# Even layer's normed heads: attention weights transposed by the DMA as halfword planes instead of by TensorE

## The reference

```python
proj = jnp.einsum('bsd,de->bse', u, w_in_even[i])
qa, ka, va, qb, kb, vb, gate = jnp.split(proj, even_splits, axis=-1)
qa = apply_axial_rope(rms_norm_2(qa.reshape(b, s, A_HEADS, HEAD_DIM), a_q_norm_g[i]), rope_tables)
ka = apply_axial_rope(rms_norm_2(ka.reshape(b, s, A_KV_HEADS, HEAD_DIM), a_k_norm_g[i]), rope_tables)
ya = gqa_attention(qa, ka, va)          # softmax(q k / sqrt(128)) v, 8 heads, 2 key/value heads
yb = diff_attention(...)                # 8 differential heads
y = jnp.concatenate([ya, yb], axis=-1) * jax.nn.silu(gate)
h = h + jnp.einsum('bse,ed->bsd', y, w_out_even[i])
```

## Time and profile before

| | us |
|---|---|
| median of 3 runs | 3058.57 (3057.92 to 3058.85) |
| the profiled execution | 3058.66 |
| its span, first to last instruction | 3056.9 |
| TensorE busy | 3043.0 |
| VectorE busy | 1869.1 |
| ScalarE busy | 1469.8 |
| POOL busy | 134.2 |

### The profile page before, as it was taken

One profiled execution on the slowest core, in us unless ns is written; L12 is line 12 of the kernel. 1 busy time (PEld: TensorE's weight loads), 2 busy tenths in 40 slices (PEclk: granted clock), 3 DMA queues, 4 the chain that ended last, 5 costly groups with the idle time before them and its releaser, 6 DMA issues.

```text
span 3056.9 us, 48305 instructions
## 1 busy us (share of the span) xinstructions
PE 3043.0 (100%) x20906; PEld 2827.8 (93%) x20906; DVE 1869.1 (61%) x2263; ACT 1469.8 (48%) x1699; POOL 134.2 (4%) x132
## 2 busy tenths in 40 slices
PE   9999999999999999999999999999999999999999
PEld 9989999999999999989888888889998889999987
DVE  7775555445445557776565565556787666767663
ACT  5544433333333357755443443345565654555553
POOL 0001000000000011110000000002000001101000
PEclk9999999999999999999999999999999999999999
DMA  6334555555554554455555555554444545555554
GB/s 236 108 111 166 174 173 178 179 177 171 176 179 168 182 195 176 159 193 179 194 191 188 185 179 198 187 192 179 179 140 153 178 175 184 179 193 186 174 191 152
DMA packets 94516, 539.57 MB, mean 177 GB/s; under 512 B 25568, under 2 KB 26080, under 8 KB 31584
## 3 DMA queue, kind: packets, MB, share of 16 engines
q1 hardware_dynamic: 77264, 532.14, 50.0%
q10 hardware_dynamic: 17040, 4.34, 0.8%
HBM read 530.15 MB, written 2.10 MB: 174 GB/s over the span
## 4 chain that ended last, share of the span: by engine, by line
PE 97%; DVE 1%; ACT 1%; DMA 1%; issue 0%; SPq 0%; ACTq 0%; DVEq 0%
PE PB L1158 28%; PE PB L1159 15%; PE PB L1183 14%; PE PB L1182 14%; PE PB L1184 13%; PE PB L1177 2%; PE PB L1178 2%; PE PB L1179 2%; PE PB L1169 1%; PE PB L1168 1%; PE PB L1167 1%; PE PB L1240 1%; DMA raw<-in_mla_in 1%; PE PB L1308 1%; DVE WLt L1796 0%; PE PB L1309 0%
## 5 line engine op out<-in xcount | busy, mean ns | idle before, releaser
L1796 DVE TENSOR_TENSOR WLt<-raw,WHt 128x2048 fp32r<-128x2048 f32 (+2 forms) x506 | 1139.3, 2259 | 760.7 <-ACT WHt L1415 760.2
L1415 ACT ACTIVATE WHt<-raw 128x2048 fp32r<-128x2048 f32 (+2 forms) x506 | 955.0, 1890 | 1117.3 <-PE PB L1159 582.0
L1158 PE MATMUL PB<-Xt,WHt 128*128 128x512 f32 x2880 | 1027.6, 395 | 0.0
L1159 PE MATMUL PB<-Xt,WLt 128*128 128x256 f32 x2880 | 808.5, 281 | 0.0
L1158 PEld LDWEIGHTS PB<-Xt,WHt 128*128 128x128 f32 x2880 | 540.8, 188 | 109.8
L1182 PE MATMUL PB<-Xt,WHt 128*128 128x272 f32 (+1 forms) x2192 | 635.0, 290 | 2.8 <-DVE WLt L1796 1.9
L1183 PE MATMUL PB<-Xt,WHt 128*128 128x272 f32 (+1 forms) x2192 | 630.2, 287 | 0.0
L1184 PE MATMUL PB<-Xt,WLt 128*128 128x272 f32 (+1 forms) x2192 | 626.9, 286 | 0.0
L1159 PEld LDWEIGHTS PB<-Xt,WLt 128*128 128x128 f32 x2880 | 543.5, 189 | 0.1
L1182 PEld LDWEIGHTS PB<-Xt,WHt 128*128 128x128 f32 x2192 | 412.8, 188 | 12.6 <-DVE WLt L1796 4.9
L1183 PEld LDWEIGHTS PB<-Xt,WHt 128*128 128x128 f32 x2192 | 413.5, 189 | 1.1 <-issue 0.2
(11 more groups left out here) (268 smaller groups left out, 2858.1 us busy)
## 6 DMA issues: line engine op xcount, KB each, us to landing
raw<-in_gu SPq DMA_DIRECT2D x176, 1024.0 KB, 4.8
raw<-in_dn SPq DMA_DIRECT2D x88, 1024.0 KB, 4.8
raw<-in_odd_in SPq DMA_DIRECT2D x64, 1024.0 KB, 4.8
raw<-in_even_in SPq DMA_DIRECT2D x52, 1024.0 KB, 4.9
raw<-in_lru_in SPq DMA_DIRECT2D x24, 1024.0 KB, 4.9
raw<-in_mla_o SPq DMA_DIRECT2D x16, 1024.0 KB, 4.8
raw<-in_lru_o SPq DMA_DIRECT2D x16, 1024.0 KB, 5.0
raw<-in_even_o SPq DMA_DIRECT2D x16, 1024.0 KB, 4.9
```

The costliest lines, as they stand in the source:

```text
L1158: t.matmul(o, wh, both, start=first, stop=False)
L1159: m = t.matmul(o[:, 0, :], wl, ah, start=False, stop=last)
L1415: a.activation(hi, r, ACT.Copy).then_inc(s_hi, 1)
L1796: v.tensor_tensor(lo, r, hi.bitcast(f32), sub).then_inc(s_lo, 1)
```

## The change

In the eight normed heads of the even layer the weights of a head are no longer transposed by TensorE. ScalarE copies them as two planes of halfwords into `EVEN_PLANES` (`even_planes`), a DMA on ScalarE's queue transposes them into `EVEN_CROSSED` (`even_cross`), two ScalarE copies put the halves together in `EVEN_WOVEN`, a third rounds them to `TTH`, and VectorE takes the rest to `TTL` (`even_weave`). Both planes are woven by ScalarE, where the odd layer has one on VectorE and the split into planes on POOL. `E1` is free once the planes are copied.

The steps of group q stand elsewhere. Head 2q: planes at the end of unit 2, crossing inside unit 3 before block 2, weave at the end of unit 4, values at the end of unit 5. Head 2q + 1: scores inside unit 3 before block 2, planes at the end of unit 4 (behind the next group's `q_step`; for q = 3 on their own), crossing at the end of unit 5, ahead of the values of head 2q, weave at the end of unit 6, values inside unit 7 before block 1. `weigh_split` now waits for `TTL`. The functions `halfwords`, `weigh_split` and `q_step` are otherwise as before.

```diff
@@ plan @@
+    def even_planes(hd):
+        p.mark("even planes", "even planes", hd)
+        p.step("even_planes", hd)
+        now["E1"] = ("even planes", hd)
+
+    def even_weave(hd):
+        p.mark("even woven", "even woven", hd)
+        p.mark("trh", "trh", hd)
+        p.mark("trl", "trl", hd)
+        p.step("even_weave", hd, now["TT2"])
...
-        p.step("weigh_split", hd, vj, ("out", "tr", hd) if stage_[0] == "e" else ("trl", hd), vready)
+        p.step("weigh_split", hd, vj, ("trl", hd), vready)
...
             rope2(("qA", q), "q", q_in)
+            if q:
+                even_planes(("e", 2 * q - 1))
...
         p.after(0, q_step)
+        a, b = ("e", 2 * q), ("e", 2 * q + 1)
         if q == 0:
             p.inside(2, 1, lambda s=s: s(0))
         else:
             p.after(1, lambda s=s: s(0))
-        p.inside(3, 1, lambda s=s, q=q: (t_step(("e", 2 * q)), s(1)))
-        p.after(4, lambda v=v, q=q: (v(0), t_step(("e", 2 * q + 1))))
-        p.after(5, lambda v=v: v(1))
+        p.after(2, lambda a=a: even_planes(a))
+        p.inside(3, 2, lambda s=s, a=a: (p.step("even_cross", a), s(1)))
+        p.after(4, lambda a=a: even_weave(a))
+        if q == 3:
+            p.after(4, lambda b=b: even_planes(b))
+        p.after(5, lambda v=v, b=b: (p.step("even_cross", b), v(0)))
+        p.after(6, lambda b=b: even_weave(b))
+        p.inside(7, 1, lambda v=v: v(1))
@@ buffers @@
+        EVEN_PLANES, EVEN_CROSSED, EVEN_WOVEN = sqt[:, 0:512], acct[:, 0:512], buf["vA"]
+        s_even_crossed = ctx.enter_context(nc.semaphore("s_even_crossed"))
@@ TensorE, steps inside a unit @@
-                elif what == "turn_split":
-                    turn(a[0])
+                elif what == "weigh_split":
+                    weigh_split(*a)
@@ ScalarE @@
+            def even_planes(hd):
+                a.wait_ge(*when("pp", hd))
+                if hd[1]:
+                    a.wait_ge(s_even_crossed, 16 * hd[1])
+                a.activation(EVEN_PLANES.bitcast(u16).rearrange("p (a n) -> p a n", a=2), halfwords(E1),
+                             ACT.Copy).then_inc(sems["even planes"], 1)
+
+            def even_cross(hd):
+                a.wait_ge(*when("even planes", hd))
+                if hd[1]:
+                    a.wait_ge(*when("even woven", ("e", hd[1] - 1)))
+                x = EVEN_CROSSED.bitcast(u16).rearrange("p (g n) -> p g n", n=128)
+                a.dma_start(x, EVEN_PLANES.bitcast(u16), transpose=True).then_inc(s_even_crossed, 16)
+
+            def even_weave(hd, free):
+                a.wait_ge(s_even_crossed, 16 * (hd[1] + 1))
+                if hd[1]:
+                    a.wait_ge(*when("trl", ("e", hd[1] - 1)))
+                for i in range(2):
+                    x = EVEN_CROSSED.bitcast(u16)[:, 512 * i:512 * i + 512].rearrange("p (q k n) -> p k q n", q=2, k=2)
+                    w = EVEN_WOVEN.bitcast(u16).rearrange("p (k q n a) -> p a k q n", k=2, q=2, a=2)[:, i]
+                    m = a.activation(w, x, ACT.Copy)
+                m.then_inc(sems["even woven"], 1)
+                a.wait_ge(*when(*free))
+                a.wait_ge(*when("even woven", hd))
+                a.activation(TTH, EVEN_WOVEN, ACT.Copy).then_inc(sems["trh"], 1)
@@ VectorE @@
+            def even_weave(hd, free):
+                v.wait_ge(*when("trh", hd))
+                v.tensor_tensor(TTL, EVEN_WOVEN, TTH.bitcast(f32), sub).then_inc(sems["trl"], 1)
```

More of the change, by code:

```diff
@@ L1733, in _ @@
                     crossed(*x)
+                elif what == "even_planes":
+                    even_planes(*x)
+                elif what == "even_cross":
+                    even_cross(*x)
+                elif what == "even_weave":
+                    even_weave(*x)
                 elif what == "uq_out":
```

## The result

The changed kernel takes 3087.53 us (median of 4 runs, 3085.28 to 3088.86), the kernel before beside it 3058.24 (3057.31 to 3058.85): 1.0095 times as long, 95% interval 1.0083 to 1.0107. The prediction said slower, 3076.4 us and at most 3085: the direction is right, the size is not.

A forecast was written before the change was run, and what follows sets the result against it. TensorE was taken as the bound, busy 3043.0 of 3056.9 us. Transposes -3.5, old waits -0.7 and -0.2, values' waits +14.9, scores' waits +7.2 gave +17.7 us: 3076.4, range 3067 to 3085 (own forecast 3071 to 3082).

The forecast's parts named there:

- Each forecast wait: TensorE waits 3.6 us three times and 4.1 once before second heads' values, and 2.4 three times before first heads' scores.
- Only the waits of v: Rival: VectorE finishes its low part before the roots come, so the scores' 7.2 us falls away: 3069.2 us; 10 in 100.
- the other sign: Rival: second head's values and the scores don't wait, so only the gain of 4.2 us is left: 3054.5; 4 in 100.
- worth of the transposes: 32 TensorE transposes removed from the eight normed heads, 0.44 us per four, win 3.5 us.
- The clock falls in the waits: Rival: each of four waits for values puts TensorE's next unit at 1.2 GHz: +22.6 us, to 3099; 6 in 100.
- Other moves: Later scores, the release of E1 and SP's loads shift no wait of TensorE; nothing added to the sum.
- With each period 5 us longer, ScalarE and VectorE gain time: In the periods between groups, these two engines gain time because each period grows by 5 us.
- ScalarE becomes the bound: Rival: ScalarE about 81% busy per period; if lateness grows between groups, some 5 us more: 3081; 8 in 100.

The follow-up runs named there:

- E1: Not a run: a buffer of the kernel, free once ScalarE has copied the planes; it has no measured time of its own.
- the kernel with the roots first: Changed kernel with the first head's weave moved behind the next pair's roots and rotation on all engines (q = 1, 2, 3): 3080.32 us, 1.0075 times before.
- The two kernels with later values: Changed kernel with the second head's values before the unit's last quarter, or after the whole unit, instead of before the second quarter: 3085.41 and 3084.69 us.
- the waits filled: Changed kernel with 26 unread matmuls put in front of each wait for the second head's values: 3085.96 us, 1.0093 times before.
- the values after the whole unit: Changed kernel with the second head's values at the end of unit 7 instead of inside it before block 1: 3084.69 us, 1.0089 times before.

## Why the prediction was right and wrong

**Direction, and the waits: right.** Each forecast wait was met within 0.5 us; the sums are 14.2 for 14.9 and 7.1 for 7.2 us. The chain that gave them (boundary, weight copy, two halfword copies, rounding, low part) stands in ScalarE's rows as it was laid out. That the scores wait because the roots stand behind the first head's weave was shown by the kernel with the roots first, with the lists of ScalarE and VectorE changed together. "Only the waits of v" is refuted, and so is the other sign. The row of before also gave the right worth of the transposes: 32 at 0.11 us fit the ledger within 1.2 us, while at 0.275 us each the ledger would come out at 22.5, 4.1 under what was measured.

**"The clock falls in the waits" was taken for a rival of 6 in 100, with the forecast expecting 1.00.** This step failed, with 8.5 us. It was argued against with "the waits are short and TensorE is full around them"; no row of before has a wait of more than 0.6 us between full stretches in these 140 us, so the rows could not say that. What they had was the fall at the end. The size was wrong on the other side: the rival let the clock be low for a whole unit, 5.64 us per wait, while here the clock was back before the unit ended and a fall cost 1.7. The Trainium skill, "TensorE: Matmul & The Clock Gate", HAM oscillation, which says that idle gaps between bursts bring the lower clock back, agrees with the trace at the four waits of the values and the bank wait, and not at the three waits of the scores.

**The bank of head 7 was not looked at.** The part "Other moves" went over the releases of E1, the scores and SP's loads, and not over the banks, though values that come later release their bank later: this step failed too, with 2.4 us that the sum put at nothing. For seven heads that costs nothing in the changed kernel, for the eighth 2.4 us, and its fall of the clock 1.7 more.

**"With each period 5 us longer, ScalarE and VectorE gain time" is wrong in kind.** It holds for busy time, but VectorE's idle time stands at fixed places of its list, in front of the weave's low part, and what is behind doesn't gain by it. The two kernels with later values showed the consequence: I expected that taking a wait away gives back its length, and it gave back nothing. The period of a pair, from scores to scores, is 34.2 us in the kernel after (2228.66 to 2262.88), where about 32 was written, and 33.4 (2228.83 to 2262.26) with the values' waits removed. The rival "ScalarE becomes the bound" was nearest to this, but it named busy time, and ScalarE is busy 105.7 of 170 us (2190 to 2360), so it isn't full. Its lateness doesn't grow from pair to pair either: 3.42, 3.70, 3.44.

**The sum.** One rounding is off: 5.09 less 1.42 is 3.67 and not 3.6, which would have made the waits for values 15.1 and the forecast 17.9. 17.7 forecast; less 0.8 for waits that were shorter, plus 8.5 of clock and 2.4 of bank makes 27.8; 26.6 was measured in the profiled execution and 29.3 between the medians.

**What stays open.** Why the sum of waits and lost clock stays at 30 to 32 us is argued from the timelines: between the boundary ahead of the second head's weave and the next pair's scores the work goes to and fro between ScalarE and VectorE with hardly a gap that TensorE could shorten. It would be tested by putting the weave's copies ahead of the weight copy on ScalarE, or the low part behind the scaling on VectorE. No run here measured either, nor a kernel in which both kinds of wait are filled. What decides whether the clock falls after a given wait is open too. No version here is faster than the kernel before.

## What to carry to other kernels

A wait put into a matrix engine that was full costs its length and can bring a slower clock behind it: here five of eight waits of 2.2 to 3.7 us brought 1.7 us each. Where an engine takes its list in order, look for the late event in every list, not only in that of the bound engine, and ask what stands behind it there; taking the wait away where it showed only moved it here, to other things that this engine releases, banks above all. When a consumer is put later, follow its bank to the next user, for each instance by itself, the last one above all.

## What the runs showed of the hardware

- The granted clock fell to 0.50 (1.2 GHz) after waits of 1.81 to 5.15 us in a TensorE that was otherwise full, and came back by itself. A lone fall costs 1.7 us; behind the longest waits the loss by the windows is two or three times that (3.4 us behind the bank wait of 3.98 with the waits filled). The length of the wait alone doesn't decide: 2.16 us before scores had no fall in the kernel after (2262.88), and the same 2.16 us before the same scores had one with the values after the whole unit (2262.01; 0.50 in the window from 2264 us); 3.42 us before the values had one in the kernel after and none with the roots first.
- The fall can come behind the restart, or in the wait itself. In the kernel after TensorE starts at 2240.23, the next matmuls are at full spacing, and the slow ones begin at 2241.05, 0.8 us behind. In the kernel with filled waits the scores at 2261.96 are slow at once (1.09 us for two against 0.67). With the values after the whole unit the clock is 0.50 in the window from 2346 us, in which TensorE runs nothing.
- A transposing DMA of 128x1024 halfwords from SBUF to SBUF landed in 3.1 us (median of eight, 3.0 to 6.5), against 2.7 for the odd layer's; the weave's first copies (L1659) never stood idle for one.
- ScalarE copies 1024 halfwords per partition in 1.04 us, but 512 with strides in 0.76, so the larger copy is the cheaper one per element (1.0 against 1.5 ns).
